# Scaling the attention probabilities on ScalarE, with a reciprocal for each partition, in place of one VectorE multiplication of two operands

## The reference, cut to what matters

```
scores = jnp.einsum('bnqhgd,bnkhd->bnhgqk', q, kb).astype(jnp.float32) * (HEAD_DIM ** -0.5)
...
scores = jnp.where(valid[None, :, None, None], scores + bias, NEG_INF)
...
probs = jax.nn.softmax(jnp.concatenate([scores, sink], axis=-1), axis=-1)[..., :-1]
out = jnp.einsum('bnhgqk,bnkhd->bnqhgd', probs.astype(v.dtype), vb)
```

## Time and profile before

| | |
|---|---|
| median of 3 runs | 2502.53 us (2500.46 to 2507.02) |
| the profiled execution | 2507.68 us |
| its span in the profile | 2505.9 us |
| mean granted clock of TensorE | 0.987 |
| PE busy | 2386.8 us, 95% |
| DVE busy | 1277.2 us, 51% |
| ACT busy | 693.3 us, 28% |
| POOL busy | 752.0 us, 30% |
| the attention loop, from scores(0) to the end of the last L1166 | from 2232.2 to 2382.5 us of the span |

### The profile page before, as it was taken

How to read it: one execution, slowest core, us unless ns; L and a number is a source line. 1 busy time by engine, 2 the same in 40 slices (tenths; PEclk the granted TensorE clock), 3 DMA queues, 4 the chain that set the end, 5 groups by cost and what they waited for, 6 DMA issues and landing times.

```text
span 2505.9 us, 33582 instructions
## 1 busy us (share of the span) xinstructions
PE 2386.8 (95%) x12944; PEld 1927.5 (77%) x12944; DVE 1277.2 (51%) x1446; ACT 693.3 (28%) x1076; POOL 752.0 (30%) x397
## 2 busy tenths in 40 slices
PE   4999999999999999898999999999999999989895
PEld 3788878887887788787787788888878787767674
DVE  6543353426433543765547644554441487737723
ACT  3422221213213222433233211111132454024421
POOL 1311231122123112113365433333334445312132
PEclk9999999999999999999999999999999999999897
DMA  3211111121112114644444111111124332111011
GB/s 120 72 46 60 60 51 60 44 76 51 51 51 68 59 51 140 227 140 160 176 126 151 52 49 50 42 50 42 50 92 138 114 118 89 54 51 43 26 42 67
DMA packets 59663, 201.01 MB, mean 80 GB/s; under 512 B 6048, under 2 KB 10272, under 8 KB 58912
## 3 DMA queue, kind: packets, MB, share of 16 engines
q1 hardware_dynamic: 39408, 134.56, 17.3%
q10 hardware_dynamic: 20144, 64.80, 7.0%
HBM read 163.16 MB, written 36.18 MB: 80 GB/s over the span
## 4 chain that ended last, share of the span: by engine, by line
PE 80%; DVE 11%; ACT 3%; DVEq 3%; issue 2%; ACTq 0%; DMA 0%; POOL 0%; POOLq 0%
PE psg L446 10%; PE psg L451 10%; PE psg L450 10%; PE psg L579 5%; PE psg L577 5%; PE psg L572 5%; PE psa L669 1%; PE psg L1110 1%; PE psg L1115 1%; PE psb L658 1%; PE psg L1117 1%; PE psa L509 1%; PE psb L665 1%; PE psg L536 1%; DVE rw_SC L1348 1%
## 5 line engine op out<-in xcount | busy, mean ns | idle before, releaser
L387 POOL CAST whi<-wraw 128x1024 fp32r<-128x1024 f32 (+1 forms) x168 | 180.2, 1072 | 1531.5 <-PE psg L572 558.6
L389 POOL TENSOR_TENSOR wlo<-wraw,whi 128x1024 fp32r<-128x1024 f32 (+1 forms) x168 | 443.8, 2642 | 26.2 <-issue 6.3
L446 PE MATMUL psg<-xhi,whi 128*128 128x512 f32 x1120 | 446.7, 399 | 2.0 <-issue 1.6
L451 PE MATMUL psg<-xhi,wlo 128*128 128x512 f32 x1120 | 443.5, 396 | 0.0
L450 PE MATMUL psg<-xlo,whi 128*128 128x512 f32 x1120 | 440.1, 393 | 0.0
L577 PE MATMUL psg<-xlo,whi 128*128 128x512 f32 x640 | 260.6, 407 | 0.0
L579 PE MATMUL psg<-xhi,wlo 128*128 128x512 f32 x640 | 260.6, 407 | 0.0
L572 PE MATMUL psg<-xhi,whi 128*128 128x512 f32 x640 | 258.5, 404 | 0.0
L451 PEld LDWEIGHTS psg<-xhi,wlo 128*128 128x128 f32 x1120 | 210.3, 188 | 52.6
L446 PEld LDWEIGHTS psg<-xhi,whi 128*128 128x128 f32 x1120 | 210.3, 188 | 52.5 <-issue 3.2
L450 PEld LDWEIGHTS psg<-xlo,whi 128*128 128x128 f32 x1120 | 210.3, 188 | 52.2 <-issue 1.0
(11 more groups left out here) (579 smaller groups left out, 4556.9 us busy)
## 6 DMA issues: line engine op xcount, KB each, us to landing
wraw<-w SPq DMA_DIRECT2D x216, 512.0 KB, 3.6
later_scratch<-stage ACTq DMA_DIRECT2D x40, 512.0 KB, 2.6
xres<-xt ACTq DMA_DIRECT2D x4, 1024.0 KB, 10.5
RV<-later_scratch SPq DMA_DIRECT2D x4, 1024.0 KB, 12.0
RG<-later_scratch SPq DMA_DIRECT2D x4, 1024.0 KB, 5.9
later_scratch<-rstage ACTq DMA_DIRECT2D x8, 512.0 KB, 2.6
mgr<-later_scratch ACTq DMA_DIRECT2D x8, 512.0 KB, 3.6
mgt<-later_scratch ACTq DMA_DIRECT2D x8, 512.0 KB, 4.5
```

Source lines behind the costliest of these rows:

```text
L387: pool.tensor_copy(whi[:, u, 0:width], wraw[:, u, 0:width])
L389: pool.tensor_tensor(wlo[:, u, 0:width], wraw[:, u, 0:width], whi[:, u, 0:width].bitcast(F32), ALU.subtract).then_inc(w_ready, 1)
L446: mm = pe.matmul(ps[:, cols], whi[:, slot, w_cols], rhs_hi(k, cols), start=(k == 0), stop=False)
L451: mm = pe.matmul(ps[:, cols], wlo[:, slot, w_cols], rhs_hi(k, cols), start=False, stop=(k == kts - 1))
```

## The change

DVE no longer multiplies the probabilities: behind the reciprocal it raises a new semaphore `a_inv` and goes on to the next step. ACT waits for `a_inv` directly behind its exponentials and multiplies the four tiles itself, each by an Identity activation of 128x256 whose scale is one column of `sm`; the last of them raises `ap_ready`. The new wait and the four activations stand ahead of everything else that ACT does in the step. A semaphore of the retention is merged with another one (`rgn_exp` into `hd_exp`, with a higher count), which keeps the number of semaphores; who waits for whom there is the same as before.

```diff
@@ -807,7 +807,7 @@
             def ret_spread(p, h):
-                pe.wait_ge(sem("rgn_exp"), 2 * p + h + 1)
+                pe.wait_ge(sem("hd_exp"), 2 * PAIRS + 2 * p + h + 1)
                 spread(RE[h]).then_inc(sem("rgn_rep"), 1)
@@ -1459,7 +1459,7 @@
                     v.tensor_copy(by_token(RE[h]), sm[:, cols].unsqueeze(2).broadcast_to([P, NB, P])
-                                  ).then_inc(sem("rgn_exp"), 1)
+                                  ).then_inc(sem("hd_exp"), 1)
@@ -1906,10 +1906,7 @@
                 v.wait_ge(sem("ae_ready"), n + 1)
                 tt(sm[:, 20:24], sm[:, 16:20], sm[:, 12:16], ADD)
                 v.drain()
-                v.reciprocal(sm[:, 20:24], sm[:, 20:24])
-                v.drain()
-                tt(pr[:, :, :], pr[:, :, :], sm[:, 20:24].unsqueeze(2).broadcast_to([P, 4, 256]), MUL
-                   ).then_inc(sem("ap_ready"), 1)
+                v.reciprocal(sm[:, 20:24], sm[:, 20:24]).then_inc(sem("a_inv"), 1)
             cat_low(2)
             cat_low(3)
             attended(4 * PAIRS - 1)
@@ -2396,6 +2393,10 @@
                     act(ap_[:, n % 2, q, :], ap_[:, n % 2, q, :], EXP, bias=sm[:, 8 + q:9 + q],
                         accum_out=sm[:, 16 + q:17 + q])
                 act(sm[:, 12:16], sm[:, 12:16], EXP).then_inc(sem("ae_ready"), 1)
+                s.wait_ge(sem("a_inv"), n + 1)
+                for q in range(4):
+                    mm = act(ap_[:, n % 2, q, :], ap_[:, n % 2, q, :], IDN, scale=sm[:, 20 + q:21 + q])
+                mm.then_inc(sem("ap_ready"), 1)
                 if n == 4 * PAIRS - 2:
                     s.wait_ge(sem("pool_done"), 4)
                     s.wait_ge(g_full, T_P2 + 18)
```

## The result

| | before | changed |
|---|---|---|
| median | 2504.82 us (15 runs, 2500.46 to 2508.90) | 2510.30 us (15 runs, 2506.69 to 2513.37) |
| ratio, 95% interval | | 1.0022 (1.0015 to 1.0030) |
| the profiled execution, its span | 2507.68, 2505.9 us | 2511.41, 2509.6 us |
| DVE busy | 1277.2 us | 1259.1 us |
| ACT busy | 693.3 us | 719.1 us |

The change costs 5.5 us by the runs (3.8 to 7.5), 0.22%. Before and behind the attention loop nothing moved: the first scores start at 2232.03 instead of 2232.17 us, and from the first matmul of the last projection to the end of the span it is 123.5 us in both profiles. All of the profiles' difference, 3.83 us, lies in the loop.

The account below looks back on a forecast made before the run. PE was taken to bound the middle of the loop, and to wait for the softmax at its end. 1.35 + 0 + 2.55 = 3.9 us slower (1.2 to 6.6) gave a median of 2506.4 us, range 2500 to 2512 us.

Parts of the forecast that it names:

- The price of the activations: ACT's four scaling activations: 1.7 us in all, between 1.25 and 2.0 us.
- no overlap: Upper bound for ACT's four scaling activations: 4 x 0.50 = 2.0 us.
- Steps on the path: Steps 0, 14 and 15, where PE waits for the scaling: 0.45 us later each, 1.35 us (0 to 2.25).
- Steps just in time: Steps 1 to 13: up to 0.46 us late costs nothing, excess 0.45; 0 us, upper bound 0.9 us.
- The sigmoid: Steps 4, 8 and 12: load and sigmoid stand behind the scaling, values 0.85 us later each; 2.55 us (1.2 to 3.45).
- DVE's relief: Attention loop: 19.6 us of DVE work go away, but PE covered it or ACT has it on the path; 0 us.
- the roundings in step 14: The early `high`, two roundings of about 1 us, moves behind the scaling; costs nothing under PE's 1.98 us of transposes.
- TensorE's clock: Rival, 12%: the clock falls after idle time; one stretch more gives 2507.9 us, three give 2510.9 us.
- all hidden: Rival, 10%: activations run at the lower bound and the table load is overlapped; 2502.5 to 2503.7 us.
- DVE's relief pays: Rival, 6%: DVE's late work keeps PE from its pace; up to 19.6 us go, 2482.9 us.
- More than the upper bound: Rival, 6%: the four activations cost over 2.0 us; from 2.1 us the sum is above 7.5 us, 2510 us and more.

Follow-up runs that it names:

- ACT in these steps alone: Kernel before, with ACT scaling only in steps 0, 14 and 15; one run with the profile, 2510.36 us, loop 151.91 us.
- ACT in the other ten: Kernel before, with ACT scaling only in steps 1, 2, 3, 5, 6, 7, 9, 10, 11 and 13; ratio 1.0005 (0.9995 to 1.0015).
- scaling twice: Changed kernel, with the four scaling activations made twice and a drain between; ratio 1.0095 (1.0079 to 1.0110) against the kernel before.
- ACT in 4, 8 and 12: Kernel before, with ACT scaling only in steps 4, 8 and 12; one run with the profile, 2506.61 us, loop 150.99 us.
- tanh: Changed kernel, with the gate's sigmoid written as 0.5 + 0.5 tanh(x / 2); ratio 1.0003 (0.9994 to 1.0012) against the kernel before.
- sigmoid first: Changed kernel, with the gate's sigmoid moved ahead of the wait for `a_inv`; one run with the profile, 2506.51 us, loop 153.09 us.
- semaphore only: Kernel before, with only the retention's semaphore merged into `hd_exp`; ratio 0.9996 (0.9987 to 1.0005).
- first two better loops: Kernel before, with `cat_low` of tiles 0 and 1 moved behind step 15's multiplication, ratio 0.9997; the same with the gate by tanh, 0.9993.
- one tile: Changed kernel, with only the first of the four tiles scaled; ratio 0.9984 (0.9974 to 0.9993) against the kernel before.
- scaling shared: Kernel before with `cat_low` moved later and gate by tanh, DVE and ACT scaling two tiles each in steps 0, 14, 15; ratio 0.9986.
- remainders later: Kernel before, with `cat_low` of tiles 0 and 1 moved behind the multiplication in step 15; ratio 0.9997 (0.9985 to 1.0008).

## Why the prediction was right, and where it was off

The direction and the mechanism held, and the size within the range, near its upper end. The forecast was 3.9 us slower, and the runs say 5.5 and 5.3 (intervals 3.8 to 7.5 and 3.0 to 7.5); the two profiles differ by 3.83 us in the loop. As an absolute time the forecast was 2506.4 and the median is 2510.30 us; 2.3 of that difference is the kernel before itself, whose median is 2504.82 over 15 runs and was 2502.53 over three. Point by point:

*The price of the activations.* 1.7 us for four was taken, 1.70 to 1.71 measured; 0.497 us each. The step held, and the bound of "no overlap" was not needed.

*Steps on the path.* 0.45 each was forecast. The pieces say 0.43 (step 14), 0.44 (step 15) and 0.43 (step 0) in the changed kernel. With ACT in these steps alone it is 0.43 in each; in step 0 that is 10.08 us from scores(0) to the transposes, against 9.65 with ACT in the other ten, which had the same short L1907.

*Steps just in time.* 0 was forecast, with 0.46 us to spare against 0.45 of excess. It came out that close: in step 4 PE's weight load waited 0.22 us for ACT, and the transposes still came on time. The kernel with ACT in the other ten steps, among them 2, 6 and 10, has no wait of PE beyond the three of before. That the other steps have more slack was true of 5, 9 and 13 by little: scaling twice shows 0.25 us left in them.

*The sigmoid.* 2.55 us was forecast as three times 0.85; 2.51 measured with ACT in 4, 8 and 12 alone, and gone with tanh. That the row of scaling, load, sigmoid and copy is the cause, and within it the load and the waiting for the reciprocal, is shown by these two kernels and by the one with the sigmoid first.

*DVE's relief.* 0 was forecast, and the ten steps alone confirm it.

*What was mis-sized.* Two things are missing in the sum. Both come from taking one profile for the loop: in that profile step 14 ran at the lower clock, and the prediction wrote that steps 14 and 15 "are at the lower one already". The same loop ran step 14 at the upper clock in "semaphore only".

The first is the roundings in step 14, put at nothing because they end while PE transposes for 1.98 us. That cover is there at the lower clock only. In the changed kernel run again the transposes took 1.09 us (2369.93 to 2371.02), and the copy came behind the roundings:

```profile
2369.78 1.99 ACT L1949 ACTIVATE xhi<-cat 128x1024 fp32r<-128x1024 f32 x2
2371.68 1.00 ACT L2414 ACTIVATE apt<-psb 128x1024 f32<-128x1024 f32 x1
```

In "semaphore only", with the same fast transposes, ACT had been idle ahead of the copy:

```profile
2365.92 1.02 ACT L2413 ACTIVATE apt<-psb 128x1024 f32<-128x1024 f32 x1 [1.97 <-PE psb L1158]
```

From transposes 14 to values 14 this is 2.80 against 2.20 us. The 2.80 stands in three of the five kernels in which ACT scales all four tiles of step 14 once (changed again, sigmoid first, tanh), and in no kernel in which DVE does. So the term is 0 to 0.6 us, by the clock.

The second is TensorE's clock ("one stretch more gives 2507.9 us" was a rival with 12%). The pieces of the loop that hold nothing but steps 0 and 14 show it. From scores(0) to values 13, less the loss of the sigmoid in the kernels that have it (2.53, or 1.81 with the sigmoid first), the six profiles in which DVE multiplies in step 0 (before, semaphore only, ACT in 4, 8 and 12, the other ten, and the first two better loops) have 129.7 to 130.0, mean 129.8. The five in which ACT scales all four tiles there once (changed, again, ACT in 0, 14, 15, sigmoid first, tanh) have 130.1 to 131.7, mean 130.8. The excess of 0.44 explains less than half of that 1.0. The rest comes from two of the five (changed again, tanh): their low stretch around scores(1) was followed by a second one behind transposes 0, about 1.6 us more. The other nine have one of the two. From values 13 to values 14, where 0.44 is due as well, the means are 8.67 and 9.45; most of the other 0.3 is the roundings. From values 14 to transposes 15 four profiles of the first kind have 5.5 or 6.4, mean 5.95, and all five of the second kind 6.83. Beyond the three times 0.44 that is 0.6 + 0.3 + 0.4 = 1.4 us, about 0.3 of it roundings and the rest clock, and 3.9 + 1.4 = 5.3 us is what the runs say. In the changed kernel run again, the values of step 14 were slow although its transposes were not:

```profile
2369.93 1.09 PE L1158 MATMUL psb<-mat,ap__181 128*128 128x128 f32 x8 [2.31 <-ACT ap__181 L2398]
2372.73 1.98 PE L1166 MATMUL psb<-apt,vt 128*64 128x128 f32 x16 [1.71 <-ACT apt L2414]
```

Does the longer wait of PE bring the clock down? In step 14 the profiles line up with it. With 2.31 us ahead of the transposes the values were at the lower level in five of five; with 1.87 or 1.88 in three of six; with 1.11 (one tile) and 1.51 (scaling shared) in neither; with 4.08 (scaled twice) they were. In step 0 they do not: a low stretch came behind waits of 1.95, 2.00, 3.24, 3.25 and 3.68 us, and none behind 1.56, 2.94, 3.34 and 3.39. The mean granted clock of the runs is 0.9879 for the changed kernel (27 runs) and 0.9886 for the one before (35 runs), which has the right sign, but "semaphore only", whose loop is the same as before, has 0.9895. So a clock that the change itself lowers is indicated for step 14 and not shown: no run changed the clock by itself, five of five against three of six can be chance, and the interval of the ratio also holds the 3.9 us without it. That the sum comes out at 5.3 is partly luck.

Of the other rivals, "all hidden" and "DVE's relief pays" are refuted. "More than the upper bound" did not occur, but scaling twice shows where it would have gone: a scaling of 3.5 us costs 18 us more.

## What to carry to other kernels

Work that is moved to an idle engine is priced by its place in that engine's order, not by the engine's busy share: here ACT was 28% busy, and two thirds of the forecast loss came from a table load and a sigmoid that had stood in ACT's idle time and were pushed behind a new wait. Ask of each instruction behind a new wait what it used to hide in, and whether that cover is there in every run: one profile of before had slow transposes over the roundings, another of the same loop did not. Where two engines can do the same operation and it stands on the path, share it in just those steps and leave the others alone; and before that, look whether something that could wait stands on the path.

## What the runs showed of the hardware

POOL's cast of the weights (L387) took 2.12 us in six of the steps before and takes 1.04 us now. The timelines of POOL, in step 4 before and changed:

```profile
2277.15 2.12 POOL L387 CAST whi<-wraw 128x1024 fp32r<-128x1024 f32 x1 [13.24 <-PE psg L1110]
```

```profile
2277.46 1.04 POOL L387 CAST whi<-wraw 128x1024 fp32r<-128x1024 f32 x1 [14.34 <-PE psg L1110]
```

Before, it began at the same moment as DVE's multiplication of two operands (2277.15), and was longer by 1.08 us, which is most of that instruction's 1.23. The other way round a DVE operation on 4 columns (L1907 in step 0) took 2.32 us beside POOL's subtraction, and 0.16 us elsewhere. The kernel before, and the one with ACT in the other ten steps, whose step 0 has the same code one line further down:

```profile
2239.12 2.32 DVE L1907 TENSOR_TENSOR sm<-sm 128x4 f32<-128x4 f32 x1 [2.24 <-ACT sm L2398]
```

```profile
2242.53 0.27 DVE L1908 TENSOR_TENSOR sm<-sm 128x4 f32<-128x4 f32 x1 [2.24 <-ACT sm L2402]
```

This agrees with the Trainium skill ("SBUF — State Buffer", section "SBUF: two separate sides"): a DVE operation with two inputs in SBUF and a POOL operation that reads SBUF take turns on one pair of ports, and whichever has it keeps it for its whole instruction. It cost PE nothing in the middle of the loop, in either kernel. In step 0 it costs 1.23 us. In nine of the fourteen profiles scores(1) took 2.08 us at the lower clock, POOL's cast began 5.7 us after scores(0), and its subtraction met L1907. In the other five (ACT in 0, 14, 15, ACT in the other ten, scaled twice, one tile, remainders later) scores(1) took 1.13 us, the cast began 4.5 us after scores(0), and L1907 took 0.27 us. For the two kernels shown, scores(0) to transposes 0 is 10.88 and 9.65 us. So a low clock of TensorE reached PE again by way of POOL and DVE.
